# An encoder trunk with expert-choice experts: two token tiles of the last expert's sum formed on the chip, and four orders changed

## The reference, cut to what matters

```
h = rmsnorm(x); x = x + mixers(h)
aff = softmax(rmsnorm(x) @ w_router); gate, idx = top_k(aff.T, cap)
xe = h[idx]                                   # per expert
ye = (silu(xe @ wg) * (xe @ wu)) @ wd * gate
x = x + zeros.at[idx].add(ye)
x = x + sigmoid(rmsnorm(x) @ w_ple_gate) * (p @ w_ple_proj)
```

## Time and profile before

| | |
|---|---|
| median of three runs | 2875.24 us (2874.88 to 2875.36) |
| the profiled execution's own time | 2874.68 us |
| its span, first to last instruction | 2872.6 us |
| PE busy | 2783.7 us, 97% of the span |
| DVE, ACT, POOL busy | 1991.6, 1587.9, 329.0 us |
| PE's share of the chain that ended last | 90% |
| mean granted TensorE clock | 0.988 of 2.4 GHz |

### The profile page before, as it was taken

One profiled execution on the slowest core, in us unless ns is written; L12 is line 12 of the kernel. 1 busy time (PEld: TensorE's weight loads), 2 busy tenths in 40 slices (PEclk: granted clock), 3 DMA queues, 4 the chain that ended last, 5 costly groups with the idle time before them and its releaser, 6 DMA issues.

```text
span 2872.6 us, 44202 instructions
## 1 busy us (share of the span) xinstructions
PE 2783.7 (97%) x15216; PEld 2268.4 (79%) x15216; DVE 1991.6 (69%) x2596; ACT 1587.9 (55%) x2268; POOL 329.0 (11%) x309
## 2 busy tenths in 40 slices
PE   8999999999899999998999999999998999999978
PEld 7998988888767777775899989888886777777756
DVE  4138884466488888887541579744755888888874
ACT  3323344343378888887442243442534888888864
POOL 1031000034001111110010300000421011111000
PEclk9999999999999999999999999999999999999989
DMA  6122222165499999999230222222645999999971
GB/s 192 38 55 65 65 78 78 58 191 196 188 346 386 386 386 382 386 386 329 100 93 25 68 65 65 82 78 68 205 168 215 370 387 387 386 384 387 387 267 52
DMA packets 309643, 605.43 MB, mean 211 GB/s; under 512 B 20076, under 2 KB 140748, under 8 KB 309392
## 3 DMA queue, kind: packets, MB, share of 16 engines
q1 hardware_dynamic: 297328, 563.81, 54.4%
q0 software_dynamic: 12192, 39.93, 5.5%
HBM read 547.04 MB, written 56.62 MB: 210 GB/s over the span
## 4 chain that ended last, share of the span: by engine, by line
PE 90%; DVE 6%; DVEq 1%; ACT 1%; issue 1%; DMA 1%; ACTq 0%; SPq 0%; POOLq 0%
PE PS L1831 20%; PE PS L1833 20%; PE PS L1832 19%; PE PS L1860 19%; PE PS L1811 3%; PE PS L1960 2%; PE PS L1949 1%; PE PS L2052 1%; DVE flo L1264 1%; PE PS L2176 1%; PE PS L2066 1%; DVE zacc L1413 1%; PE PS L2095 1%; PE PS L2109 1%; PE PS L1934 1%
## 5 line engine op out<-in xcount | busy, mean ns | idle before, releaser
L1259 DVE TENSOR_TENSOR wlo<-raw,whi 128x1024 fp32r<-128x1024 f32 (+2 forms) x872 | 1027.5, 1221 | 353.2 <-ACT whi L817 345.0
L817 ACT ACTIVATE whi<-raw 128x1024 fp32r<-128x1024 f32 (+2 forms) x872 | 889.0, 1046 | 308.3 <-PE PS L1833 297.8
L1860 PE MATMUL PS<-hT,fhi 128*128 128x512 f32 (+1 forms) x2048 | 453.3, 343 | 0.7
L1831 PE MATMUL PS<-whi,xeT 128*96 128x512 f32 x1024 | 404.8, 395 | 3.1 <-DVE xeT L1269 3.1
L1833 PE MATMUL PS<-whi,xeT 128*96 128x512 f32 x1024 | 403.2, 394 | 0.0
L1832 PE MATMUL PS<-wlo,xeT 128*96 128x512 f32 x1024 | 401.3, 392 | 0.0
L1831 PE MATMUL PS<-whi,hT 128*128 128x432 f32 (+1 forms) x960 | 361.5, 377 | 3.5 <-DVE wlo L1259 2.1
L1832 PE MATMUL PS<-wlo,hT 128*128 128x432 f32 (+1 forms) x960 | 356.9, 372 | 0.0
L1833 PE MATMUL PS<-whi,hT 128*128 128x432 f32 (+1 forms) x960 | 356.9, 372 | 0.0
L1860 PEld LDWEIGHTS PS<-hT,fhi 128*128 128x128 f32 x2048 | 316.4, 189 | 44.7 <-issue 1.9
L1860 PE MATMUL PS<-hT,flo 128*128 128x512 f32 (+1 forms) x1024 | 263.9, 339 | 0.0
(11 more groups left out here) (282 smaller groups left out, 3623.9 us busy)
## 6 DMA issues: line engine op xcount, KB each, us to landing
raw<-in_w_gate_e SPq DMA_DIRECT2D x256, 512.0 KB, 9.1
raw<-in_w_up_e SPq DMA_DIRECT2D x256, 512.0 KB, 8.1
raw<-in_w_down_e SPq DMA_DIRECT2D x256, 512.0 KB, 8.9
raw<-in_w_in SPq DMA_DIRECT2D x64, 512.0 KB, 4.3
raw<-in_w_in SPq DMA_DIRECT2D x48, 432.0 KB, 4.6
gate_logits<-raw SPq DMA_DIRECT2D x32, 384.0 KB, 2.7
gate_logits<-fout SPq DMA_DIRECT2D x32, 384.0 KB, 2.7
gates<-gate_logits SPq DMA_DIRECT2D x32, 384.0 KB, 5.5
```

What stands on the lines that cost most here:

```text
L817: A(whi[slot % SPLIT][:, 0:w], raw[slot][:, 0:w], ACT.Copy).then_inc(s_hi, 1)
L1259: V.tensor_tensor(wlo[j % SPLIT][:, 0:w], raw[j % slots][:, 0:w], whi[j % SPLIT][:, 0:w].bitcast(F32), ALU.subtract).then_inc(s_lo, 1)
L1831: nc.tensor.matmul(out, x[0], w[0], start=first, stop=False)
L1860: m = nc.tensor.matmul(PS[:, bb, 0:(t1 - t0) * 128], w[wn], x[xn](t0, t1), start=first and p == 0, stop=last and p == 2)
```

## The change

- The loops over experts run over 15, and the last expert is written out behind them, without gather and transposes for a next one.
- A row of the numbers 0 to 255 is loaded from the constants (`token`), compared on DVE with the last expert's indices (`idx_l`), and gives a float32 matrix of zeros and ones, 96 rows by 256 tokens (`hot`). PE multiplies it with ye in four products of 512 columns (`back`), and DVE adds them to the rows of tiles 0 and 1 (`add_back`).
- Rows of tiles 0 and 1 are reloaded after the fifteenth expert's scatter, between the fourth and the fifth fetch of the gate weights. The last scatter, unchanged in size, waits for these two reloads. Tiles 2 to 5 are reloaded after it.
- ye moves to memory that the gates use later; its old place holds `token` and `hot`.
- Opening: tile 2's square and norm go ahead of tile 1's eviction. Layer 2: the fourth weight split goes ahead of the last gate (ACT) and of its product (DVE). The table is loaded behind the first tile's zlT copies.

The diff, without the renamed semaphores and the changed counts (17 gathers become 16):

```diff
+    c[:, K_TOK:K_ALL] = np.arange(NBK * 128)
...
-        ye = moe("ye", [CAP, D])
+        ye = at("ye", [CAP, D], M0 + 4 * 8192 + 4 * 2048)
+        token = moe("token", [CAP, NBK * 128])
+        hot = moe("hot", [CAP, NBK * 128])
...
                 sp.wait_ge(s_rt, l * NT + NT)
+                sp.dma_start(token[:], consts[0:CAP, K_TOK:K_ALL]).then_inc(s_pin, 16)
...
-                for j in range(8):
+                def load_pg(j):
+
                     sp.wait_ge(s_lo, l * SPL + (S_P + j - RING + 1 + RAW))
                     fetch(j, wpg_f, l * D + j % 4 * 256, 2, j // 4 * 512, 512)
+
+                def reload(t):
+
+                    sp.dma_start(rows[:, t, :], x_d[t * 128:(t + 1) * 128, :]).then_inc(s_xin[t], 16)
+
+                for j in range(4):
+                    load_pg(j)
+                sp.wait_ge(s_sca, l * 256 + 240)
+                for t in range(NBK):
+                    reload(t)
+                for j in range(4, 8):
+                    load_pg(j)
                 sp.wait_ge(s_sca, l * 256 + 256)
-                for t in range(NT):
-                    sp.dma_start(rows[:, t, :], x_d[t * 128:(t + 1) * 128, :]).then_inc(s_xin[t], 16)
+                for t in range(NBK, NT):
+                    reload(t)
...
+                nc.gpsimd.tensor_copy(idx_s[:], idxT[:, NE - 1:NE])
+                pool.drain()
+                for t in range(NBK):
+                    wait(s_xin[t], (2 * l + 3) * 16)
+                add_rows(NE - 1)
+                wait(s_sca, l * 256 + 256)
...
+            act.wait_ge(s_xin[2], 16)
+            norm_square(0, T_N0, 2)
+            root(2)
             norm_hi(0, T_N0, 1)
-            for t in range(2, 3):
-                act.wait_ge(s_xin[t], 16)
-                norm_square(0, T_N0, t)
-                root(t)
...
-                act.preload_act_table_set("natural_log_exp_and_others")
...
+                        if n == 0:
+                            act.preload_act_table_set("natural_log_exp_and_others")
...
+                            if last:
+                                act.wait_ge(s_sca, l * 256 + 240)
                             wait_alone(act, s_used, done)
                             for c in range(2):
                                 A(ye[:, c * 512:(c + 1) * 512], PS[0:CAP, 4 + c, :], ACT.Copy,
-                                  scale=gateT[:, bass.ds(e, 1)]).then_inc(s_y, 1)
+                                  scale=gateT[:, NE - 1:NE] if last else gateT[:, bass.ds(e, 1)]).then_inc(s_y, 1)
...
-                for t in range(2):
-                    act.wait_ge(s_xin[t], (2 * l + 3) * 16)
+                for t in range(NBK):
+                    act.wait_ge(s_taken, l * (P_DVE + NBK) + P_DVE + t + 1)
                     norm_square(l, T_N2, t)
                     root(t)
...
-                    for n in range(3):
+                    for n in range(4):
                         w_hi(l + 1, n)
                     gate(1, 5)
                     norm_hi(l + 1, T_N0, 1)
-                    w_hi(l + 1, 3)
...
+            norm_out(0, 0, 2)
             norm_lo(0, T_N0, 1)
-            norm_out(0, 0, 2)
...
+                def add_back(t):
+
+                    dve.wait_ge(s_xin[t], (2 * l + 3) * 16)
+                    for c in range(2):
+                        dve.wait_ge(s_unit, l * (2 * (NT - 1) + 2 * NBK) + 2 * (NT - 1) + 2 * t + c + 1)
+                        r = rows[:, t, c * 512:(c + 1) * 512]
+                        m = V.tensor_tensor(r, r, PS[:, 2 * t + c, :], ALU.add)
+                    m.then_inc(s_taken, 1)
...
+                        if s == 12 and last:
+                            dve.wait_ge(s_pin, l * 48 + 48)
+                            V.tensor_scalar(hot[:], token[:], idx_l[:, 0:1], None, ALU.is_equal)
...
+                        if s == 23 and last:
+                            add_back(0)
                         lo(l * SPL + e * ES + (S_E + s + 4), s + 4, 1024, RING)
...
+                with dve.Fori(0, NE - 1) as e:
+                    expert_dve(e, False)
+                expert_dve(NE - 1, True)
+
+                for t in range(1, NBK):
+                    add_back(t)
                 norm_out(l, 2, 0)
...
-                    for n in range(1, 3):
+                    for n in range(1, 4):
                         w_lo(l + 1, n)
                     gated(1, 5)
                     norm_lo(l + 1, T_N0, 1)
-                    w_lo(l + 1, 3)
...
+                def back(t, c):
+
+                    pe.wait_ge(s_y, l * 32 + 30 + c + 1)
+                    nc.tensor.matmul(PS[:, 2 * t + c, :], hot[:, t * 128:(t + 1) * 128], ye[:, c * 512:(c + 1) * 512],
+                                     start=True, stop=True).then_inc(s_unit, 1)
+
+                for t in range(NBK):
+                    for c in range(2):
+                        back(t, c)
...
                 def g_free(c):
-                    return lambda t: (s_ea, l * AAPL + (AA_P + 6 * (c - 1) + t + 1 + 6))
+
+                    if c == 0:
+                        return lambda t: (s_taken, l * (P_DVE + NBK) + P_DVE + min(t // 2 + 1, NBK))
+                    return lambda t: (s_ea, l * AAPL + (AA_P + t + 1 + 6))
```

More of the change, by code:

```diff
@@ L86 @@
 T_E = T_N1 + 12
-T_N2 = T_E + 4 * NE + 2
+T_N2 = T_E + 4 * NE
 TPL = T_N2 + 12
@@ L102 @@
 K_N = K_RC + 2 * 4 * HD
+NBK = 2
+K_TOK = K_N
+K_ALL = K_TOK + NBK * 128
 def shape_constants():
-    c = np.zeros((128, K_N), np.float32)
+    c = np.zeros((128, K_ALL), np.float32)
+    c[:, K_TOK:K_ALL] = np.arange(NBK * 128)
     i = np.arange(128)
@@ L779, in _, with add_rows @@
                                         in_offset=bass.IndirectOffsetOnAxis(ap=idxT[:, 0:1], axis=0)).then_inc(s_ga, 16)
-                with pool.Fori(0, NE) as e:
+                def add_rows(e):
+                    wait(s_y, l * 32 + e * 2 + 2)
+                    pool.indirect_dma_start(out=x_d, out_offset=bass.IndirectOffsetOnAxis(ap=idx_s[:, 0:1], axis=0),
+                                            in_=ye[:], in_offset=None, compute_op=ALU.add).then_inc(s_sca, 16)
+                with pool.Fori(0, NE - 1) as e:
                     nc.gpsimd.tensor_copy(idx_s[:], idxT[:, bass.ds(e, 1)])
                     wait(s_tp, l * TPL + e * 4 + (T_E + 2))
-                    wait(s_ga, l * (17 * 16) + e * 16 + 16)
+                    wait(s_ga, l * (16 * 16) + e * 16 + 16)
                     nc.gpsimd.tensor_copy(idx_g[:], idxT[:, bass.ds(e + 1, 1)])
@@ L789, in _ @@
                                             ).then_inc(s_ga, 16)
[L790 to L792 removed]
+                    add_rows(e)
                     wait(s_sca, l * 256 + e * 16 + 16)
+                nc.gpsimd.tensor_copy(idx_s[:], idxT[:, NE - 1:NE])
[4 more added lines that the diff above has]
+                wait(s_sca, l * 256 + 256)
                 wait(s_xn, l * 18 + 18)
@@ L1153, in _, with expert_act @@
                 e_hi(3)
-                with act.Fori(0, NE) as e:
+                def expert_act(e, last):
                     for s in range(ES):
@@ L1166, in _ @@
                             t_hi(j + 1, hidT[0][:, 4:8, :], tbank(1, 4, CAP))
-                        if s == 19:
+                        if s == 19 and not last:
                             t_hi(j + 2, xeT[0][:, 0:4, :], tbank(0, 4, CAP))
-                        if s == 21:
+                        if s == 21 and not last:
                             t_hi(j + 3, xeT[0][:, 4:8, :], tbank(1, 4, CAP))
                         if s == 23:
+                            if last:
+                                act.wait_ge(s_sca, l * 256 + 240)
                             wait_alone(act, s_used, done)
@@ L1724, in _, with expert_dve @@
                     lo(l * SPL + (S_E + n), n, 1024, RING)
-                with dve.Fori(0, NE) as e:
+                def add_back(t):
[5 more added lines that the diff above has]
+                    m.then_inc(s_taken, 1)
+                def expert_dve(e, last):
                     for s in range(ES):
@@ L2251, in _, with expert_pe @@
                 pe.wait_ge(s_pp1, l * P_ACT + P_ACT)
-                with pe.Fori(0, NE) as e:
+                def expert_pe(e, last):
                     tl = l * TLL + e * 4 + (T_E - 12 + 2 + 2)
@@ L2265, in _ @@
                     row_steps(e, 16, 2, 2, 4, hidT)
-                    pe.wait_ge(s_ga, l * (17 * 16) + e * 16 + 32)
-                    transposes(None, 0, [xe[:, k * 128:(k + 1) * 128] for k in range(4)], (s_tlo, tl + 1), CAP)
+                    if not last:
+                        pe.wait_ge(s_ga, l * (16 * 16) + e * 16 + 32)
+                        transposes(None, 0, [xe[:, k * 128:(k + 1) * 128] for k in range(4)], (s_tlo, tl + 1), CAP)
                     pe.wait_ge(s_tlo, tl + 2)
                     row_steps(e, 16, 4, 2, 4, hidT)
-                    transposes(None, 1, [xe[:, k * 128:(k + 1) * 128] for k in range(4, 8)], (s_tlo, tl + 2), CAP)
+                    if not last:
```

(10 more changed lines are left out.)

28 lines of the change are left out of this document (16 added, 12 removed).

## The result

The changed kernel takes 2852.62 us in the median of four runs (2851.17 to 2853.71), against 2875.22 of the kernel before: a ratio of 0.9921, 95% interval 0.9904 to 0.9938. That is 22.6 us off, where 21.2 were forecast (2854.0 us); the time lies in the range. The profiled execution took 2851.17 us, its span is 2849.4.

What follows compares the result with a forecast made beforehand. The prediction took PE's waits as what the kernel can still lose. Savings of 15.4 + 2.4 + 1.5 + 1.9 = 21.2 us from 2874.68 gave 2853.5, plus 0.56 for the median: 2854.0 us, range 2848.9 to 2860.4.

Steps and rivals of the forecast that it cites:

- The end of a layer: Behind the last expert: PE resumes at about 7.1 us instead of 14.14, plus 0.66 of dropped work; 7.7 us per layer.
- The mis-sized term: Added float32 products at layer ends: 512 columns cost some 0.5 us each, taken from a row of 256-column products.
- The side calculation: If one float32 product took 1.03 us, DVE's row would reach 6.05 instead of 5.5, losing 0.3 us more per layer.
- The end that was counted to: Layer ends: the saving was counted up to the start of tile 0's transposes, about 7.1 us instead of 14.14.
- What hides the rest: Tiles 2 to 5, reloaded after the scatter: nearly 4 us of cover before tile 2's transposes, some 2 after tile 1's eviction.
- The rival that the stall moves to tile 2: Layer ends: half of each layer's saving comes back as a wait at tile 2; 2861.7 us, 8%.
- The clock: Behind the layer-end gap: the clock falls as today, no change, since the empty 4.1 us exceed 3.7 us.
- the clock stays up: Rival: the level stays high at both layer ends, 4.6 us faster in all; 2849.4 us, 12%.
- Opening, layer 2, table: Small orders: opening saves 2.4 us (tile 2's earlier norm), layer 2's fourth split 1.5, table behind the zlT copies 1.9.
- The small orders give nothing: Rival: in the opening, layer 2 and at the table the next wait takes the removed one's place; 2859.8 us, 8%.
- The sum: Whole kernel: 15.4 + 2.4 + 1.5 + 1.9 = 21.2 us saved, giving 2854.0 us.
- The slower rival: Layer ends: the low clock lasts after PE resumes; at 40 us per layer the time would be 2887 us; 3%.

Runs made afterwards that it cites:

- e4: The changed kernel with three more float32 products, which nothing reads, behind the four added ones; 2848.58 us.
- e6: The changed kernel with ye and hot in fp32r, so that the four added products are single passes; 2851.66 us.
- e5: The changed kernel with tile 0's norm put ahead of tile 1's adds on DVE; 2856.64 us.
- e7: The changed kernel with only tile 0 added on chip; tile 1 is reloaded behind the scatter and squared ahead of tile 0's eviction; 2864.24 us.
- e1: The kernel before with the small orders alone (opening, layer 2's splits, place of the table), layer ends as before; 2866.23 us.
- e2: The changed kernel with the small orders put back, so only tiles 0 and 1 added on chip; 2860.08 us.
- e3: The changed kernel run again without any edit; 2853.03 us.

## Why the prediction was right, and where it was off

*The end of a layer.* Right: 7.7 us per layer forecast; by tile 2's transposes 25.06 − 18.41 = 6.65 in layer 1 and 24.84 − 18.30 = 6.54 in layer 2, and with the 0.66 of dropped transposes ('s price; PE's timelines of the two kernels move 0.68 and 0.70 us apart over the last expert) 14.5 for both, 15.4 forecast. The wait, where it stands, what splits it and the four products in it are as described.

*The mis-sized term* is the float32 product: "four products of 512 columns … one product is some 0.5 us", read from the row of four 256-column records in 1.03 us. A record is not a product. That line has 48 records for 24 products, as the code counts them (2 layers, 6 tiles, 2 products each), and the added products stand as eight records for four. In e4 six records of the same form with nothing between them take 2.74 us at 0.59 for the last, so one comes every (2.74 − 0.59)/5 = 0.43 us and a product takes 0.86. The same reading of the earlier trace rows, (1.03 − 0.38)/3 = 0.22 per record (0.38 us is one record's own time in that line's group), so 0.43 for 256 columns, would have given 0.87 for 512.

The Trainium skill, page "FP8 and Floating Point Precision", section "TensorE Precision Notes", says that true float32 takes four passes. The trace agrees: 0.86 us against the 0.23 from one expert product to the next is a factor of 3.7. The side calculation that went with that rule put DVE's row at 6.05 us to tile 0's norm instead of 5.5; measured is 1348.24 − 1342.21 = 6.03, and the gap is 7.37, not 7.1. That the row meets 6.05 so closely is in part luck: tile 0's add ended at 3.55 (1345.76 − 1342.21) and not at 3.2, because the first product holds PE until 0.83 + 0.86 = 1.69, past the second half of ye, and what stands behind the add took 2.5 us instead of 2.85. So the 0.3 us per layer that this rule was to cost are what is missing at tile 0, and e6 shows the counterpart: with a single pass the gap is 6.90 and ACT's row holds the norm, as the forecast had it.

*The end that was counted to* was tile 0's transposes. That served because before and after have 2.6 us from there to tile 1's. e5 shows that it need not: earlier at tile 0, slower in all.

*What hides the rest.* Right. Tile 2's transposes have no wait. Its norm ends at 1355.94, that is 13.7 us after the last product, and PE gets there at 18.41: 4.7 us of cover, nearly 4 forecast. The rival that the stall moves to tile 2 falls, and e7 shows how it looks when the cover is taken away. The comparison took 0.34 us (0.3 forecast), and PE has no wait for a split in the last expert.

*The clock.* Right in the outcome, "a fall as today and no change": 6.8 us of low level behind the gap, where it was 6.7. The reason given failed, and the outcome was luck: it was that the empty part, 4.1 us by the forecast, "alone is longer than those 3.7 us". The products lasted longer than forecast, so the empty part was 2.83 us, shorter than 3.7; by that reason the level would have stayed, and it fell all the same. The rival "the clock stays up" did not come with this change, but e4 made it so with three idle products, and its price was right: 4.6 us forecast, 4.3 by the traces, 4.45 by the medians. The parts of that price were not: of layer 1's 2.2 us only 0.2 lie between tile 0's and tile 1's transposes (2.59 against 2.36 in e4), since PE then waits longer for tile 0's eviction, and 2.0 between tile 1's and tile 2's (8.45 against 6.46).

*Opening, layer 2, table.* 2.4, 1.5 and 1.9 us forecast; 2.6, 1.8 and 2.3 by e1's trace. In the opening the forecast's own two ends, 21.2 and 23.9, lie 2.7 apart; it took 2.4 and gave no reason. The table's upper bound of 1.9, the sum of the waits, was too low: the stretch became 1.1 us shorter in each layer, where the waits were 0.98 and 0.93. Where the rest came from was not tried. "The small orders give nothing" falls by e1.

*The sum.* 14.5 + 6.7 = 21.2 by the traces' pieces, 21.2 forecast; measured 22.6 and, in another session, 21.3. The two measurements differ by 1.3, about what the forecast missed in the first. The 23.5 us between the two profiled executions hold some 2.6 that are not the change's. Of these, 1.2 are there by tile 1's transposes in the opening (18.05 and 16.86). Some 0.3 come behind layer 1's top-k, where the low level held 13.7 and 10.2 us. And 1.1 are left by a low stretch of 3.4 us in layer 2's mixers that fell in the one execution and not in the other: PE's timelines lie 15.1 us apart ahead of it and 16.2 behind. *The slower rival*, a low clock that lasts, did not happen.

## What to carry to other kernels

A stall through memory can be shortened by doing only the first tiles on the chip, as many as it takes to cover the long way of the rest (here two; one left 6 us per layer uncovered, three were not tried): count the cover to the last tile that the next stage needs before it can run, not to the first. Where PE stands still for a few microseconds, ask what the clock does behind the gap; work that nobody reads can be worth more than an earlier start. Before a row is used as the price of an instruction, count its records against the code.

## What was not expected of the hardware

- A gap on PE of 2.5 us was followed by transposes at the upper level in one execution (2.52, then 1.09 us) and at the lower in another (2.53, then 1.83 us, e2); 2.37 us (e5) by the upper in layer 1 (1.09) and by the lower in layer 2 (1.97), 2.83 us by a fall ahead of the transposes or during them in all three profiled executions that have that gap, at both layer ends, 1.27 us (e4) by the upper.
- The level also fell for 3.4 us in a stretch in which PE was busy throughout (3.40 of 3.40 us, e3), in four of the ten profiled executions (before, e1, e3, e7) and not in the others. Ahead of it PE was busy too (2.40 of 2.40 us in e3), mostly with products of 64 columns; in the first execution of the changed kernel the same products were not followed by a fall.
- Filling 2.6 of 2.83 idle microseconds made each layer 2.1 to 2.2 us shorter without any instruction starting earlier in the gap.
